# First mixer of a two-block network on Trainium2: token products moved between the steps of the triangular inverse

## The chip, the cores and the metric

The kernel is one program on one core of a Trainium2 chip. The metric is the device time of one execution in microseconds (us), given as a median of several runs. The core's engines run side by side, each through its own queue in order: PE (TensorE, matrix products and transposes into PSUM banks of 512 floats in each of 128 partitions), DVE (VectorE), ACT (ScalarE), POOL (GpSimd) and SP (which only issues transfers here). They wait for each other through semaphores. PE's clock stands at one of two levels, 1.2 and 2.4 GHz; a profile calls the share granted 0.50 and 1.00.

## What is computed

Two networks run one after the other on 256 tokens of width 1024. In the first, each of two layers has a feed-forward block, a mixer, and a second feed-forward block; the second network has two layers of another mixer and a retrieval block. The change is in the mixer of the first network, which runs twice in an execution. Cut to what matters here:

```
proj = u @ w_in        # 3.5 k columns: m (4 heads of 64), r (4 of 64), g (4 of 128), gates
h_m = mlstm(mq, mk, mv, i, f);  y_m = head_rmsnorm(h_m) * sigmoid(mo)
h_r = retention(rope(rq), rope(rk), rv);  y_r = head_rmsnorm(h_r) * silu(rg)
qkv = silu(causal_dwconv(concat(gq, gk, gv), g_conv))          # four taps
q, k = l2norm(q), l2norm(k)
# gated delta rule, in chunks, for every head:
a_mat = eye + where(strict, (kb @ k.T) * decay, 0)             # unit lower triangular
sol = triangular_solve(a_mat, [v * beta, kb * exp(g)])
u = sol_v - sol_k @ S
o = (q * exp(g)) @ S + ((q @ k.T) * decay) @ u
S = exp(g_last) * S + (k * exp(g_last - g)).T @ u
y_g = head_rmsnorm(o) * silu(gz)
out = concat(y_m, y_r, y_g) @ w_out
```

## The kernel before

The kernel works in chunks of 128 tokens (two, index `b`), so the inverse has 4 heads x 2 chunks = 8 matrices of 128 x 128, kept side by side and handled in two halves of four.

**Weights** come as units of 128 x 1024 floats. SP loads unit n into one of three `ring` slots once DVE is done with unit n-3. ACT copies it to a high part (L405) as soon as PE is done with unit n-3, and DVE subtracts to get the low part (L408). PE multiplies high x high, high x low and low x high in a fast format. The `Splitter` calls `split.upto(n)` in the code of ACT and DVE say where in each queue a unit is split; a job that stands behind such a call waits until the unit's turn comes.

**PSUM**: four banks `W` are shared in strict rotation by all numbered jobs (`Group`, `claim`, `freed`): job k may start only when the reader of job k-4 has freed the bank. Four more banks, `ACC`, hold the sums of the down and output projections and lie idle in the rest of the mixer. The list `MIX1_STAGES` gives the names of the stages in order with how many jobs and units each has.

**Order of the mixer**: transposed input (`xT`), small gate columns (`small`), 16 units of channel-major products (`tt0` to `tt3`: m queries and keys, g queries, keys, values, PE L668), with the four-tap convolution of the 12 g tiles on DVE (L1584, L1586, L1588) behind them; 16 units of token-major products (`tok0` to `tok3`, PE L743) in the `W` banks; between them the sums of squares of the g queries and keys (`gss`, L803), roots on ACT (L1203), reciprocals and scaling on DVE (L1597, L1599). Then come the m scores and output (`bM`, `msc`, `mout`), the r scores and output (`rtr`, `rsc`, `rout`), transposes of g keys and values (`gtr`), rows spread over partitions (`bg`, `bb`, L815), key and query products (`gkk`), the inverse, its uses (`gout`, L921), and the output projection of 8 units (`wout`, L690).

**The inverse** (`inv`) works in LEVELS = 7 levels on `TI` and its transpose `WI`. At level n POOL multiplies all 8 matrices with a mask (`EL`, L558); PE forms EL x TI, ACT copies it to `XI` (L1268), PE forms both WI x XI and XI x WI (L910), and DVE subtracts the one from `TI` and the other from `WI` (L1696). `TI` and `WI` are both kept up to date by products.

## Time and profile before

| What | us |
|---|---|
| median of 3 runs (lowest to highest) | 3322.17 (3319.99 to 3328.34) |
| time of the profiled execution | 3336.64 |
| its span, first to last instruction | 3334.9 |
| layer 0 mixer, first `xT` transpose to the end of `wout` | 218.62 to 464.22 |
| layer 1 mixer, same | 871.08 to 1119.67 |
| token units of layer 0 | 282.6 to 341.2 |
| from the token units to the `yT` transposes, layer 0 | 343.2 to 435.2 |

A row of a timeline has a start, a duration, the engine, the line, the operation, and in brackets the idle time before it and what ended it. `x48` counts records; an f32 product that is not of the fast format leaves two records.

### The profile page before, as it was taken

What the parts mean: (1) busy time and instruction counts of PE and PEld (TensorE: products, weight loads), DVE (VectorE), ACT (ScalarE), POOL (GpSimd) and SP (SyncE); (2) the same over time, 40 slices, a digit from 0 to 9 for tenths busy, and PEclk for the clock granted to TensorE, in tenths of its full rate; (3) what the DMA queues carried; (4) which work ended last, traced back from release to release, by engine and by line L of the source; (5) the groups of instructions that cost most, each with busy time, mean ns of one, the idle gap of its engine ahead of it and who ended that gap; (6) DMA issues with size and microseconds to landing.
All of it is one profiled execution on the core that took longest, in us unless ns stands there. A gap on an engine that the chain in (4) does not pass through costs nothing.

```text
span 3334.9 us, 58740 instructions
## 1 busy us (share of the span) xinstructions
PE 3099.9 (93%) x20832; PEld 2830.3 (85%) x20832; DVE 2179.9 (65%) x3744; ACT 1533.2 (46%) x2314; POOL 449.3 (13%) x255
## 2 busy tenths in 40 slices
PE   7988889999888898879999999998879999999997
PEld 7987879989878797769999988887769999988886
DVE  4547545555574555566978867777566978867776
ACT  4445244444452444434555545454435555545543
POOL 0001300000013000113850000000103850000000
PEclk9989789999897899889999999999889999999999
DMA  5535025545340355336876567776335876677775
GB/s 198 188 127 164 20 95 183 188 153 187 127 151 1 121 188 164 124 108 180 224 218 182 182 211 241 242 239 214 115 120 178 226 215 182 182 222 240 241 242 167
DMA packets 213006, 579.56 MB, mean 174 GB/s; under 512 B 23728, under 2 KB 88528, under 8 KB 212352
## 3 DMA queue, kind: packets, MB, share of 16 engines
q1 hardware_dynamic: 209216, 562.62, 54.0%
q0 software_dynamic: 3648, 14.99, 1.3%
q8 instruction: 96, 1.57, 0.2%
q14 instruction: 46, 0.38, 0.0%
HBM read 541.34 MB, written 36.18 MB: 173 GB/s over the span
## 4 chain that ended last, share of the span: by engine, by line
PE 76%; POOL 7%; DVE 7%; issue 6%; ACT 3%; DMA 1%; POOLq 0%; SPq 0%; DVEq 0%; ACTq 0%
PE work L668 33%; PE acc L690 31%; POOL wsp L648 6%; PE work L743 5%; PE acc L1064 3%; PE work L910 2%; DVE xsp L1425 1%; DVE wsp L408 1%; ACT wsp L405 1%; PE work L766 1%; DMA ring<-in_stream 0%; PE work L921 0%; DVE h L1456 0%; PE work L842 0%; DVE h L1730 0%
## 5 line engine op out<-in xcount | busy, mean ns | idle before, releaser
L668 PE MATMUL work<-xsp,wsp 128*128 128x256 f32 x12096 | 1510.6, 285 | 13.9 <-DVE xsp L1425 6.8
L668 PEld LDWEIGHTS work<-xsp,wsp 128*128 128x128 f32 x12096 | 1481.2, 193 | 24.4 <-issue 15.9
L408 DVE TENSOR_TENSOR wsp<-ring,wsp 128x1024 fp32r<-128x1024 f32 x824 | 1010.9, 1227 | 645.7 <-ACT wsp L405 645.2
L405 ACT ACTIVATE wsp<-ring 128x1024 fp32r<-128x1024 f32 x944 | 993.6, 1053 | 601.1 <-PE work L668 275.7
L690 PE MATMUL acc<-wsp,hsp 128*128 128x512 f32 x4128 | 957.8, 391 | 11.2 <-issue 10.9
L690 PEld LDWEIGHTS acc<-wsp,hsp 128*128 128x128 f32 x4128 | 773.4, 189 | 169.4 <-issue 12.0
L648 POOL TENSOR_TENSOR wsp<-ring,wsp 128x1024 fp32r<-128x1024 f32 x120 | 304.4, 2549 | 168.7 <-ACT wsp L405 168.3
L1367 ACT ACTIVATE hsp<-arena 128x256 fp32r (+1 forms) x256 | 107.0, 418 | 360.2 <-PE acc L690 340.3
L529 POOL TENSOR_TENSOR st<-st,mhalf 128x2 f32<-128x2 f32 x12 | 13.3, 1105 | 1689.7 <-DVE st L1440 879.0
L743 PE MATMUL work<-wsp,xsp 128*128 128x512 f32 x768 | 196.0, 417 | 35.5 <-DVE wsp L408 10.7
L743 PEld LDWEIGHTS work<-wsp,xsp 128*128 128x128 f32 x768 | 154.3, 204 | 75.7 <-DVE wsp L408 13.7
L1935 DVE TENSOR_TENSOR one_hots<-iota,selT 128x512 bf16<-128x512 bf16 x256 | 97.2, 422 | 81.7 <-PE acc L1064 81.7
L1973 DVE TENSOR_TENSOR hsp<-arena,hsp 128x256 fp32r<-128x256 f32 x256 | 109.0, 426 | 57.4 <-ACT hsp L1367 57.4
L1944 DVE TENSOR_TENSOR one_hots<-one_hots,selT 128x512 bf16<-128x512 bf16 x384 | 139.6, 420 | 0.0
L1146 ACT ACTIVATE hsp<-scratch 128x256 fp32r<-128x256 f32 x88 | 36.7, 418 | 184.7 <-DVE scratch L1473 184.7
L1962 DVE TENSOR_TENSOR arena<-arena,back 128x256 f32 (+1 forms) x252 | 105.7, 419 | 22.1 <-DMA back<-acts_dram 22.0
L1138 ACT ACTIVATE scratch<-work 128x256 f32<-128x256 f32 x88 | 33.7, 383 | 167.4 <-PE work L668 167.4
L1064 PE MATMUL acc<-one_hots 128*128 128x128 bf16 x1536 | 110.2, 219 | 0.2 <-DVE one_hots L1944 0.2
L690 PE MATMUL acc<-wsp,xsp 128*128 128x512 f32 x384 | 95.5, 413 | 5.6 <-DVE xsp L1425 5.6
L679 PE MATMUL work<-cst,scratch 128*128 128x128 f32 x160 | 37.0, 425 | 67.0 <-DVE scratch L1445 47.9
L690 PEld LDWEIGHTS acc<-wsp,xsp 128*128 128x128 f32 x384 | 77.2, 202 | 23.7 <-issue 7.1
L1064 PEld LDWEIGHTS acc<-one_hots 128*128 128x128 bf16 x1536 | 88.0, 97 | 5.9 <-DVE one_hots L1944 0.4
(301 smaller groups left out, 1950.5 us busy)
## 6 DMA issues: line engine op xcount, KB each, us to landing
ring<-in_stream SPq DMA_DIRECT2D x944, 512.0 KB, 3.5
back<-acts_dram SPq DMA_DIRECT2D x252, 128.0 KB, 3.2
acts_dram<-acts SPq DMA_DIRECT2D x128, 128.0 KB, 3.6
acts_dram<-arena SPq DMA_DIRECT2D x124, 128.0 KB, 4.3
rows_sb<-in_rows POOLq DMA_DIRECT2D x10, 512.0 KB, 5.0
h_saved_dram<-h POOLq DMA_DIRECT2D x2, 1024.0 KB, 4.2
h<-h_saved_dram POOLq DMA_DIRECT2D x2, 1024.0 KB, 7.4
scratch<-in_levels POOLq DMA_DIRECT2D x3, 448.0 KB, 4.8
```

The source lines that it names most:

```text
L405: self.eng.activation(dst[:, 0, :], src, ACT.Copy).then_inc(high_done, 1)
L408: self.eng.tensor_tensor(dst[:, 1, :], src, dst[:, 0, :].bitcast(F32), ALU.subtract)\
L648: pool.tensor_tensor(dst[:, 1, :], ring[:, n % RING, :], dst[:, 0, :].bitcast(F32), ALU.subtract) .then_inc(low_done, 1)
L668: mm = pe.matmul(out_, lhsT=w[:, a, 128 * c:128 * c + 128], rhs=xsp[:, b, c, :], start=(c == 0 and n == 0), stop=(c == DC - 1 and n == 2))
L690: mm = pe.matmul(ACC[2 * b + n][:, :], lhsT=act[:, pa, 128 * b:128 * b + 128], rhs=w[:, pw, 512 * n:512 * n + 512], start=(first and m == ...
L743: mm = pe.matmul(G.bank(b)[:, :], lhsT=xsp[:, px, c, 128 * b:128 * b + 128], rhs=w[:, pw, 512 * cc:512 * cc + 512], start=(c == 0 and n == ...
L1064: mm = pe.matmul(ACC[g % 4][:, 128 * t:128 * t + 128], lhsT=slot[:, 0, t // 2, :, t % 2], rhs=slot[:, m, t // 2, :, t % 2], start=(m == 1) ...
L1367: act.activation(hsp[:, j % 2, 0, :], arena[:, bass.ds(it * (6 * T) + j * T, T)], ACT.Copy)\
L1935: ins = tt(slot[:, m], iota2.unsqueeze(1).broadcast_to([P, 2, NKEYS, 2]), spread(g, m), ALU.is_equal)
L1944: ins = tt(slot[:, m], slot[:, 1], spread(g, {1: 2, 2: 3, 3: 4}[m]), ALU.mult)
L1962: tt(a, a, back[j % 4], ALU.mult).then_inc(gated, 1)
L1973: tt(hsp[:, j % 2, 1, :], arena[:, bass.ds(it * (12 * T) + j * T, T)], hsp[:, j % 2, 0, :].bitcast(F32), ALU.subtract).then_inc(act_low, 1)
```

## The change

In words, for each of the two mixers:

- The channel units come in the order keys, values, queries, then m (`ttk`, `ttv`, `ttq`, `ttm`). ACT writes a tile twice: plain, and scaled with the last tap; DVE adds the other three taps.
- The norms of g keys and queries are no longer multiplied into the tiles. Sums of squares are products with one column of ones (`ksum`, `qsum`), POOL takes the power -1/2 of 8 numbers a partition, and the results are factors: in the decay matrix, in `beta`, in the scales with which ACT evicts the transposed keys and values (`kbe`, `vb`, `kd`), and in the last norm of the output. `gss`, the roots and the reciprocals are gone.
- `NT` is formed ahead of the token units, between the channel units.
- A level of the inverse is `mul` (NT x TI, unmasked), a masking on DVE straight from PSUM into `XI`, `add` (WI x XI), and a subtraction from `TI`. `WI` comes from `turn`, 8 transposes of `TI`, copied by ACT. POOL has no part in it. The masks are loaded transposed.
- The 16 token units accumulate in the `ACC` banks, one between two steps of the inverse or the other jobs; ACT takes a finished group of four (`taken`).
- m, r and g work is dealt out between the levels; the transposed output comes in two halves (`yT0`, `yT1`) with four units of the output projection between.

```diff
-MIX1_STAGES = [("xT", 8, 0), ("small", 1, 0), ("tt0", 4, 4), ("cums", 1, 0), ("tt1", 4, 4), ("rows", 1, 0),
-               ("tt2", 4, 4), ("mcols", 1, 0), ("tt3", 4, 4), ("tok0", 2, 4), ("tok1", 2, 4), ("gss", 4, 0),
-               ("tok2", 2, 4), ("tok3", 2, 4), ("bM", 2, 0), ("msc", 4, 0), ("mout", 2, 0), ("rtr", 4, 0), ("rsc", 4, 0),
-               ("rout", 2, 0), ("gtr", 4, 0), ("bg", 2, 0), ("bb", 2, 0), ("gkk", 4, 0),
-               ("inv", 6 * LEVELS - 6, 0), ("gout", 7, 0), ("yT", 8, 0), ("wout", 0, 8)]
+MIX1_STAGES = [("xT", 8, 0), ("small", 1, 0), ("ttk", 4, 4), ("cums", 1, 0), ("ttv", 4, 4), ("rows", 1, 0), ("ksum", 1, 0),
+               ("ttq0", 2, 2), ("bg", 2, 0), ("ttq1", 2, 2), ("mcols", 1, 0), ("brow", 1, 0), ("gkk", 2, 0),
+               ("ttm0", 2, 2), ("bb", 2, 0), ("ttm1", 2, 2), ("tok", 0, 16), ("inv0", 2, 0), ("qsum", 1, 0), ("turn0", 2, 0),
+               ("mul1", 2, 0), ("add1", 2, 0), ("bM", 2, 0), ("turn1", 2, 0),
+               ("mul2", 2, 0), ("add2", 2, 0), ("gtr0", 2, 0), ("turn2", 2, 0),
+               ("mul3", 2, 0), ("add3", 2, 0), ("msc", 4, 0), ("turn3", 2, 0),
+               ("mul4", 2, 0), ("add4", 2, 0), ("gtr1", 2, 0), ("turn4", 2, 0),
+               ("mul5", 2, 0), ("add5", 2, 0), ("rtr", 4, 0), ("mout", 2, 0), ("turn5", 2, 0),
+               ("mul6", 2, 0), ("add6", 2, 0), ("rsc", 4, 0), ("gqk", 2, 0), ("u0", 1, 0), ("uv1", 1, 0), ("wT", 1, 0),
+               ("rout", 2, 0), ("S1", 1, 0), ("u1", 1, 0), ("yT0", 4, 0), ("out0", 1, 0), ("out1", 1, 0), ("wout0", 0, 4),
+               ("yT1", 4, 0), ("wout1", 0, 4)]
...
-            n8 = NT.rearrange("p h b t -> p (h b) t")
-            G = Group(part, "inv")
-            for n in range(LEVELS):
-                if n:
-                    G.ready(pool, inverse_job(n - 1, 0, 1))
-                pool.tensor_tensor(EL, n8, lvl(n).unsqueeze(1).broadcast_to([P, 8, P]), ALU.mult)\
-                    .then_inc(ev("EL_ready"), 1)
-                if n == 0:
-
-                    pool.wait_ge(ev("W_ready"), l + 1)
...
+                def tokens(t):
+
+                    g, i = t // 4, t % 4
+                    if t == 0:
+                        acc_claim(pe, part)
+                    elif i == 0 and g >= 2:
+                        pe.wait_ge(tok_taken, 8 * l + 2 * (g - 1))
+                    w = K.unit(pe, t)
+                    for cc in range(2):
+                        c = 2 * i + cc
+                        for b in range(NB):
+                            for n, (px, pw) in enumerate(PARTS):
+                                mm = pe.matmul(ACC[2 * (g % 2) + b][:, :], lhsT=xsp[:, px, c, 128 * b:128 * b + 128],
+                                               rhs=w[:, pw, 512 * cc:512 * cc + 512],
+                                               start=(c == 0 and n == 0), stop=(c == DC - 1 and n == 2))
+                    mm.then_inc(unit_done, 1)
...
+                def head_sums(name, sq_):
+
+                    G = Group(part, name)
+                    G.claim(pe, 0)
+                    for b in range(NB):
+                        for i in range(4):
+                            mm = pe.matmul(G.bank(0)[:, 4 * b + i:4 * b + i + 1], lhsT=sq_[:, i, 128 * b:128 * b + 128],
+                                           rhs=ones[:, 0:1], start=True, stop=True)
+                    mm.then_inc(job_done, 1)
+
...
+                Group(part, "rows").freed(pe, 0)
+                spread("bg", rows8, 4, 8)
+                channels("ttq1", 2)
+
...
+                G = Group(part, "brow")
+                G.claim(pe, 0)
+                pe.wait_ge(ev("brk_ready"), l + 1)
+                for b in range(NB):
...
+                channels("ttm0", 2)
+                Group(part, "brow").freed(pe, 0)
+                spread("bb", brow, 0, 4)
+                channels("ttm1", 2)
...
+                def turn(n):
+
+                    made = inv0 if n == 0 else Group(part, f"add{n}")
+                    G = Group(part, f"turn{n}")
+                    for half in range(2):
+                        made.freed(pe, half)
+                        G.claim(pe, half)
+                        for m in range(4):
+                            mm = pe.transpose(G.bank(half)[:, 128 * m:128 * m + 128], TI[:, 4 * half + m, :], ident)
+                        mm.then_inc(job_done, 1)
...
+                def mul(n):
+
+                    made = inv0 if n == 1 else Group(part, f"add{n - 1}")
+                    G = Group(part, f"mul{n}")
+                    for half in range(2):
+                        made.freed(pe, half)
+                        G.claim(pe, half)
+                        for m in range(4):
+                            a = 4 * half + m
+                            mm = pe.matmul(G.bank(half)[:, 128 * m:128 * m + 128], lhsT=n8[:, a, :], rhs=TI[:, a, :],
+                                           start=True, stop=True)
+                        mm.then_inc(job_done, 1)
...
+                def add(n):
+
+                    masked, turned, G = Group(part, f"mul{n}"), Group(part, f"turn{n - 1}"), Group(part, f"add{n}")
+                    lhs, rhs = (WI, XI) if n < LEVELS - 1 else (XI, WI)
+                    for half in range(2):
+                        masked.freed(pe, half)
+                        turned.freed(pe, half)
+                        G.claim(pe, half)
+                        for m in range(4):
+                            a = 4 * half + m
+                            mm = pe.matmul(G.bank(half)[:, 128 * m:128 * m + 128], lhsT=lhs[:, a, :], rhs=rhs[:, a, :],
+                                           start=True, stop=True)
+                        mm.then_inc(job_done, 1)
+
...
+                turn(0)
+                mul(1)
+                tokens(1)
+                add(1)
+                spread("bM", mrow, 0, 4)
+                tokens(2)
+                turn(1)
+
+                mul(2)
+                tokens(3)
+                add(2)
+                pe.wait_ge(ev("conv_silu"), 3 * l + 2)
+                keys_values(0)
+                tokens(4)
...
+                    Group(part, "add6").freed(pe, half)
+                    Group(part, "gtr1").freed(pe, half)
+                heads("u0", lambda i: [(WI[:, 2 * i, :], vb[:, i, 0, :])])
...
+                pe.wait_ge(tok_taken, 8 * l + 6)
+                head_out("rout", rp, lambda b, i: tok[:, b, 768 + 64 * i:832 + 64 * i], 64, "rsc")
+                tokens(13)
+                Group(part, "u0").freed(pe, 0)
+                heads("S1", lambda i: [(kd[:, i, :], u0[:, i, :])])
+                tokens(14)
+                Group(part, "wT").freed(pe, 0)
+                Group(part, "S1").freed(pe, 0)
+                heads("u1", lambda i: [(wT[:, i, :], S1[:, i, :])])
+                tokens(15)
+                make_xT(part, y, "yT0", ("half_y", l + 1), 0, 4)
+                for half in range(2):
+                    Group(part, "gqk").freed(pe, half)
+                heads("out0", lambda i: [(QK[:, i, 0, :], u0[:, i, :])])
+                pe.wait_ge(ev("qe_ready"), l + 1)
+                Group(part, "u1").freed(pe, 0)
+                heads("out1", lambda i: [(qe[:, i, :], S1[:, i, :]), (QK[:, i, 1, :], u1[:, i, :])])
+                pe.wait_ge(tok_taken, 8 * (l + 1))
+                G = Group(part, "wout0")
+                for c in range(4):
+                    down_unit(G, c, xsp[:, :, c, :], c == 0, False)
+                make_xT(part, y, "yT1", ("y_ready", l + 1), 4, 4)
+                G = Group(part, "wout1")
...
+                def channel(name, q, tile):
+
+                    G = Group(part, name)
+                    split.upto(G.u + q + 2)
+                    G.ready_unit(act, q)
+                    src = G.bank(q)[:, 0:T]
+                    act.activation(cin[:, tile, 3:3 + T], src, ACT.Copy)
+                    G.free(act.activation(cT[:, tile, :], src, ACT.Copy,
+                                          scale=pr1[:, l, P_CONV + 4 * tile + 3:P_CONV + 4 * tile + 4]), q)
...
+                def turned(n):
+
+                    G = Group(part, f"turn{n}")
                     for half in range(2):
-                        job = inverse_job(n, 0, half)
-                        G.ready(act, job)
-                        G.free(act.activation(XI[:, 4 * half:4 * half + 4, :].rearrange("p a t -> p (a t)"),
-                                              G.bank(job)[:, :], ACT.Copy), job)
...
+                def conv(name, q, tile):
+
+                    G = Group(part, name)
+                    split.upto(G.u + q + 2)
+                    G.freed(dve, q)
+                    for tap in range(3):
+                        w = pr1[:, l, P_CONV + 4 * tile + tap:P_CONV + 4 * tile + tap + 1]
+                        ins = stt(cT[:, tile, :], cin[:, tile, tap:tap + T], w, cT[:, tile, :], ALU.mult, ALU.add)
+                        if tap < 2:
+                            step(ins)
+                    ins.then_inc(ev("conv_done"), 1)
...
+                conv("ttq1", 0, 2)
+                dve.wait_ge(ev("dec_exp"), 2 * l + 2)
+                for a in range(4):
+                    for b in range(NB):
+                        ins = stt(dec[:, a, b, :], dec[:, a, b, :], kn[:, b, a:a + 1], tri, ALU.mult, ALU.mult)
+                step(ins)
+                conv("ttq1", 1, 3)
...
+                G.ready(dve, 0)
+                G.free(tt(guard, cs[:, :, 0:4], G.bank(0)[:, 0:8].rearrange("p (b n) -> p b n", b=NB), ALU.add), 0)
+                G.freed(dve, 0)
+                dve.tensor_copy(guard, guard).then_inc(ev("mm_ready"), 1)
+                G = Group(part, "brow")
+                G.ready(dve, 0)
+                G.free(dve.tensor_copy(brow[0:4, :], G.bank(0)[0:4, 0:T]), 0)
...
+                def masked(n):
+
+                    for G, half, o, a in halves(f"mul{n}"):
+                        G.free(tt(XI[:, a, :], o, lvl(n).unsqueeze(1).broadcast_to([P, 4, P]), ALU.mult), half)
+
+                def subtract(n):
+
+                    buf = TI if n < LEVELS - 1 else WI
+                    for G, half, o, a in halves(f"add{n}"):
+                        if n == LEVELS - 1:
+                            Group(part, "turn5").freed(dve, half)
+                        G.free(tt(buf[:, a, :], buf[:, a, :], o, ALU.subtract), half)
```

How the instructions stand, first on PE at the token units. Before, L743 is a token unit's product (12 to a unit, so 8 units in a row of 96), L803 the sums of squares, L815 a spread, L829 and L830 the m scores:

```order
L668 MATMUL work<-xsp,wsp 128x256 x96
L743 MATMUL work<-wsp,xsp 128x512 x96
L803 MATMUL work<-scratch,cst 128x512 x4
L743 MATMUL work<-wsp,xsp 128x512 x96
L815 MATMUL work<-scratch,cst 128x256 x4
L829 MATMUL work<-scratch 128x256
```

In the changed kernel L859 makes the transposes of `inv0`, L755 is a token unit's product, L796 `qsum`, L873 a `turn`, L885 a `mul`, L899 an `add`, L811 a spread:

```order
L859 MATMUL work<-cst,scratch 128x128 x8
L755 MATMUL acc<-wsp,xsp 128x512 x12
L796 MATMUL work<-cst,scratch 128x1 x8
L873 MATMUL work<-cst,scratch 128x128 x8
L885 MATMUL work<-scratch 128x128 x8
L755 MATMUL acc<-wsp,xsp 128x512 x12
L899 MATMUL work<-scratch 128x128 x8
L811 MATMUL work<-scratch,cst 128x256 x4
L755 MATMUL acc<-wsp,xsp 128x512 x12
L873 MATMUL work<-cst,scratch 128x128 x8
L885 MATMUL work<-scratch 128x128 x8
```

The token units have moved from two blocks of eight ahead of everything to single ones between the jobs of the inverse. Next, DVE behind the last channel units. Before, L408 is a unit's low part, L1575 the reader of `mcols`, and the others the four taps:

```order
L1586 SCALAR_TENSOR_TENSOR scratch<-scratch 128x256 x2
L1588 SCALAR_TENSOR_TENSOR scratch<-scratch 128x256
L408 TENSOR_TENSOR wsp<-ring,wsp 128x1024
L1575 TENSOR_TENSOR scratch<-scratch,work 128x8
L1577 COPY scratch<-scratch 128x8
L1584 TENSOR_SCALAR scratch<-scratch 128x256
L1586 SCALAR_TENSOR_TENSOR scratch<-scratch 128x256 x2
L1588 SCALAR_TENSOR_TENSOR scratch<-scratch 128x256
```

In the changed kernel L416 is the low part, L1723 the three taps, L1774 the eight differences of the decay, L1781 its eight maskings, L1787 the reader of `mcols` and L1792 that of `brow`, whose banks the first unit behind them (`ttm0`) uses:

```order
L416 TENSOR_TENSOR wsp<-ring,wsp 128x1024
L1723 SCALAR_TENSOR_TENSOR scratch<-scratch 128x256 x3
L1774 TENSOR_SCALAR scratch<-work,scratch 128x128 x8
L416 TENSOR_TENSOR wsp<-ring,wsp 128x1024
L1723 SCALAR_TENSOR_TENSOR scratch<-scratch 128x256 x3
L1781 SCALAR_TENSOR_TENSOR scratch<-scratch,cst 128x128 x8
L416 TENSOR_TENSOR wsp<-ring,wsp 128x1024
L1723 SCALAR_TENSOR_TENSOR scratch<-scratch 128x256 x3
L416 TENSOR_TENSOR wsp<-ring,wsp 128x1024
L1787 TENSOR_TENSOR scratch<-scratch,work 128x8
L1789 COPY scratch<-scratch 128x8
L1792 COPY scratch<-work 4x256
```

The reader of `mcols` now stands behind the decay work. Last, PE from the first g results to the output projection. Before, L910 is the inverse, L921 its uses, L679 the eight transposed tiles, L690 the output projection:

```order
L890 MATMUL work<-cst,scratch 128x128 x8
L910 MATMUL work<-scratch 128x128 x136
L921 MATMUL work<-scratch 128x128 x32
L679 MATMUL work<-cst,scratch 128x128 x16
L690 MATMUL acc<-wsp,xsp 128x512 x96
```

In the changed kernel L1002 makes the uses of the inverse, L755 token units, L661 transposes, L672 the output projection:

```order
L755 MATMUL acc<-wsp,xsp 128x512 x12
L1002 MATMUL work<-scratch 128x128 x4
L755 MATMUL acc<-wsp,xsp 128x512 x12
L1002 MATMUL work<-scratch 128x128 x4
L755 MATMUL acc<-wsp,xsp 128x512 x12
L661 MATMUL work<-cst,scratch 128x128 x8
L1002 MATMUL work<-scratch 128x128 x12
L672 MATMUL acc<-wsp,xsp 128x512 x48
L661 MATMUL work<-cst,scratch 128x128 x8
L672 MATMUL acc<-wsp,xsp 128x512 x48
```

The transposes and the output projection are in two halves now, the first ahead of the last two g products.

## Rows read from the trace of the kernel before

**Rows 1.** The page: shares by engine, then the splitting of weights on DVE and ACT.
```profile
PE 3099.9 (93%) x20832; PEld 2830.3 (85%) x20832; DVE 2179.9 (65%) x3744; ACT 1533.2 (46%) x2314; POOL 449.3 (13%) x255
...
L408 DVE TENSOR_TENSOR wsp<-ring,wsp 128x1024 fp32r<-128x1024 f32 x824 | 1010.9, 1227 | 645.7 <-ACT wsp L405 645.2
L405 ACT ACTIVATE wsp<-ring 128x1024 fp32r<-128x1024 f32 x944 | 993.6, 1053 | 601.1 <-PE work L668 275.7
```
**Rows 2.** Stretches of layer 0: length, busy PE, PEld, DVE, ACT, POOL, granted clock, DMA, GB/s.
```profile
282.60:341.20 58.60, 49.74 (x202) 38.10 (x200) 39.69 (x31) 35.62 (x41) 8.99 (x6) 0.97 0.48 152
343.20:435.20 92.00, 76.95 (x497) 71.55 (x497) 45.75 (x99) 21.53 (x68) 30.37 (x18) 0.77 0.02 7
354.00:366.00 12.00, 10.48 (x51) 9.39 (x51) 6.11 (x20) 2.46 (x12) 2.42 (x3) 0.50 0.01 1
405.00:422.00 17.00, 16.63 (x147) 16.44 (x146) 8.75 (x14) 3.58 (x6) 5.64 (x3) 1.00 0.01 2
```
**Rows 3.** Timeline of PE, layer 0: transposes and weight units.
```profile
218.62 3.71 PE L679 MATMUL work<-cst,scratch 128*128 128x128 f32 x16 [6.37 <-DVE scratch L1445]
...
231.91 13.64 PE L668 MATMUL work<-xsp,wsp 128*128 128x256 f32 x96
...
247.36 11.75 PE L668 MATMUL work<-xsp,wsp 128*128 128x256 f32 x96 [0.80 <-DVE wsp L408]
...
312.86 11.13 PE L743 MATMUL work<-wsp,xsp 128*128 128x512 f32 x48 [1.31 <-ACT scratch L1203]
328.74 12.55 PE L743 MATMUL work<-wsp,xsp 128*128 128x512 f32 x48 [4.75 <-issue]
...
435.20 3.71 PE L679 MATMUL work<-cst,scratch 128*128 128x128 f32 x16 [4.17 <-DVE scratch L1524]
440.31 23.91 PE L690 MATMUL acc<-wsp,xsp 128*128 128x512 f32 x96 [1.39 <-DVE xsp L1425]
```
**Rows 4.** Timeline of PE, layer 0: small jobs of the mixer.
```profile
341.22 1.99 PE L815 MATMUL work<-scratch,cst 4*128 4x256 f32 x8
...
349.06 2.42 PE L842 MATMUL work<-scratch 128*128 128x65 f32 x10 [1.24 <-DVE scratch L1622]
...
357.96 1.23 PE L829 MATMUL work<-scratch 64*128 64x256 f32 x4 [0.83 <-ACT scratch L1246]
...
366.12 0.42 PE L866 MATMUL work<-cst,scratch 128*128 128x128 f32 x1
...
369.32 0.27 PE L867 MATMUL work<-cst,scratch 128*128 128x128 f32 x1
```
**Rows 5.** Timeline of PE, layer 1.
```profile
871.08 3.61 PE L679 MATMUL work<-cst,scratch 128*128 128x128 f32 x16 [6.35 <-DVE scratch L1445]
...
1039.68 1.10 PE L890 MATMUL work<-cst,scratch 128*128 128x128 f32 x8 [2.93 <-POOL scratch L558]
...
1095.75 23.92 PE L690 MATMUL acc<-wsp,xsp 128*128 128x512 f32 x96 [1.39 <-DVE xsp L1425]
```
**Rows 6.** Timeline of DVE, layer 0.
```profile
251.32 1.01 DVE L1586 SCALAR_TENSOR_TENSOR scratch<-scratch 128x256 f32<-128x256 f32 x2
...
371.49 2.16 DVE L1654 TENSOR_SCALAR scratch<-work,scratch 128x128 f32<-128x128 f32 x8 [1.99 <-ACT scratch L1257]
...
393.41 0.69 DVE L1696 TENSOR_TENSOR scratch<-scratch,work 128x512 f32<-128x512 f32 x1 [7.30 <-PE work L910]
394.30 0.69 DVE L1696 TENSOR_TENSOR scratch<-scratch,work 128x512 f32<-128x512 f32 x1 [0.20 <-PE work L910]
```
**Rows 7.** Timeline of POOL, layer 0: one masking of a level.
```profile
403.55 2.36 POOL L558 TENSOR_TENSOR scratch<-scratch 128x1024 f32<-128x1024 f32 x1 [3.07 <-PE work L910]
```
**Rows 8.** Timeline of ACT, layer 0: a table load, two activations of 128x1024.
```profile
240.23 1.28 ACT L1185 ACT_TABLE_LOAD   x1
...
298.11 2.01 ACT L1225 ACTIVATE scratch<-scratch 128x1024 f32<-128x1024 f32 x2
```

785 lines of the change are left out of this document (422 added, 363 removed).

## Prediction

> **What bounds the kernel now.** I read the page's shares first: PE is busy 93% of the span, so whatever shortens the time must take work or waiting from PE or raise its clock [rows 1]. The change touches only the first mixer, run twice, so the next view is the table of stretches of one mixer, and there the page's average misleads. In the token units (58.6 us) PE is at clock 0.97 and loaded with weights. In the 92.0 us behind them no weight arrives (DMA share 0.02), the clock is 0.77, and POOL is busy for 30 us. PE counts as busy for 77 us there, but part of that is at half clock: in 354 to 366 PE is busy 10.5 of 12 us at 0.50, with small products only; in 405 to 422, the products of the inverse, it is at 1.00 [rows 2]. The timeline of PE then gives the ends of a mixer: 218.62 to 440.31 + 23.91 = 464.22, so 245.6 us in layer 0, and 871.08 to 1095.75 + 23.92 = 1119.67, so 248.6 us in layer 1 [rows 3, 5]. The timelines of DVE and POOL show the loop of a level: a POOL masking of 2.36 us with 3.07 us of waiting before it, that is one level in 5.4 us [rows 7]. Of these 5.4 us PE's 24 products fill nearly all at full clock: the DVE subtractions of 0.69 us start 0.89 us apart, one job of four products each, so a product costs 0.22 us [rows 6]. The inverse is bound by PE already; what is wasted is clock and gaps around it, and the 8 products a level that only keep the transpose of `TI`.
>
> **The change: PE's work at full clock.** I rebuild a mixer as what PE must do one after the other, and add the waits afterwards.
>
> - `xT` and `small`, unchanged: 218.62 to 231.91 = 13.3 us [rows 3].
> - 16 channel units: 13.5 us for the first four, which start at low clock, then 11.75 / 4 = 2.94 each for 12 = 35.2; sum 48.7 [rows 3].
> - Between them: `cums` with its wait to the next unit as now (up to 247.36) 2.0; `rows`, `mcols`, `brow` 0.3 each = 0.9, an estimate from two transposes; `bg` and `bb` 1.99 each like `bM`, 4.0 [rows 4]; `gkk` 8 products of 0.22 = 1.8 [rows 6]. `ksum` is 8 products of one column. Nothing in the rows has that shape; it can hardly be dearer than 8 spread products of 256 columns (4.0) nor cheaper than the 1.1 of 8 transposes [rows 4, 5]; I take 2.0, near the 128-column product, as loading the weights is the same. Sum 10.7.
> - `inv0`: 8 transposes in 1.10 [rows 5]; `qsum` 2.0 as above. Sum 3.1.
> - 16 token units: 11.13 / 4 = 2.78 each at full clock, 44.5 [rows 3]. That they go to other banks changes nothing in their length.
> - The inverse: 6 `turn` of 1.1 = 6.6; 12 `mul` and `add` of 2 x 0.89 = 21.4 [rows 5, 6]. Sum 28.0, where 34 jobs of 0.89 = 30.3 stood and POOL in the loop.
> - The jobs dealt out between: `bM` 2.0, `gtr` 16 transposes 2.2, `rtr` 1.1, `gqk` 1.8, five of the g uses at 0.9 = 4.5; `mout` and `rout` have 24 records each, 2.42 / 10 = 0.24 a record at half clock, so 2.7 each at full; `msc` and `rsc`: 1.23 for two heads' wide products at half clock and the narrow ones to it, about 2.0 each at full, an estimate [rows 4]. Sum 20.9.
> - `yT0`, `yT1` 2.2, `out0` 0.9, `out1` 1.8. Sum 4.9.
> - 8 output units of the same 12 products of 512 columns as a token unit, 2.78 each = 22.2 (23.91 now, with a start at low clock [rows 3]).
>
> Sum: 13.3 + 48.7 + 10.7 + 3.1 + 44.5 + 28.0 + 20.9 + 4.9 + 22.2 = 196.3 us.
>
> **What PE waits for.** The cover of the inverse's handovers is one token unit of 2.78 us. DVE's masking is 2 x 0.69 [rows 6] behind one low part of 1.23, which itself waits for ACT's 1.05 [rows 1], released by the token unit before: 1.05 + 1.23 + 1.4 = 3.7 us, against the `turn`, `mul` and token unit in between (5.7 us): covered, as is the subtraction behind `add`, which has a small job and a token unit. Uncovered are six places:
>
> - `ksum` waits for the squares of the keys. ACT needs a table load of 1.28, `silu` and square of 1.0 each, and two evictions [rows 8], some 4.5 us against one channel unit of 2.9: 1.5 us.
> - The first `ttm0` unit claims the bank of `mcols`. DVE reads it only after 6 low parts (7.4), 5 convolutions of three taps at 0.5 (7.5) [rows 6], the row copy and scan 1.1, eight differences 2.2 [rows 6], eight maskings of the same size (2.4, an estimate from the differences), a dozen small ones 1.6, and 1.9 of waiting for POOL and ACT: 24.1 us. PE has four units (11.7), `bg`, `mcols`, `brow`, `gkk` (4.4) and about 1.0 of waiting for ACT in the same time and starts 0.8 later: 24.1 - 0.8 - 17.1 = 6.2 us of idle PE. This is the largest single wait, and nothing covers it.
> - `turn0` waits for DVE's four steps at `inv0`: 1.0 us.
> - The rotation of banks. `msc`, `rtr` and `rsc` have four jobs, so their third and fourth need the banks of the `add` just before, freed only by the subtraction, which stands behind a low part: 1.1 + 1.0 + 1.0, and `gqk` behind `rsc` 1.2. Sum 4.3.
> - `yT0` ends with a wait for its four tiles. ACT must first split a unit (1.05) and take the last token group (2 x 0.55), then 4 tiles at about 0.44: 3.6 us beyond the transposes. Now eight tiles at half clock take 435.20 to 440.31, 5.1 us [rows 3].
> - `yT1`: half of these 5.1 us, less its transposes: 1.5 us. The g norm before it (about 6 us on ACT, POOL and DVE) lies beside four output units of 11 us.
>
> Sum 18.1 us. Then the clock. Behind the idle 4.75 us four token units took 12.55 instead of 11.13, and the first channel units 13.64 instead of 11.75 [rows 3]: a fall costs 1.4 to 1.9. I count three falls (`ttm0`, the small jobs around `inv0` and `qsum`, `yT0`) at 2.0 = 6.0. Bounds: none, 0, and one for each of the 12 slots, 24.
>
> A mixer is then 196.3 + 18.1 + 6.0 = 220.4 us. Gain: 245.6 - 220.4 = 25.2 in layer 0 and 248.6 - 220.4 = 28.2 in layer 1, 53.4 us together. The profiled span of 3334.9 goes to 3281.5; against the median of 3322.2, 14 us below the profiled execution, that is **3269 us**.
>
> One rule speaks against this change. In the trace the clock rises in the midst of the 16 transposes of `gtr`: the first takes 0.42 us, the last 0.27 [rows 4]. The Trainium skill (TensorE: Matmul & The Clock Gate, Part 4: PE-mode transpose) says that the clock gate does not take transposes for activity of PE. By that rule the six `turn` would count as pauses. These rows do not bear it out plainly, since work from before may have raised the clock; the time that it would give is the second rival.
>
> **The rivals.**
>
> *Better cover.* The 6.2 us at `ttm0`, the rotation waits and the clock falls are worked out from queues. If they vanish, 5 to 6 us of waiting stay: 196.3 + 5.5 = 201.8 a mixer, gain 43.8 + 46.8 = 91 us, 3232 us. For it: PE's own products set the level period already [rows 6]. Against: DVE is in order, and its work behind the last channel units is plain to count.
>
> *Thin cover.* Each of six levels has a small fall of the clock in or after its `turn`, or a handover that is late by as much: 6 x 2.0 = 12 us a mixer more. Gain 13.2 + 16.2 = 29 us, 3293 us. For it: small products kept the clock at 0.50 for 12 us with PE nearly always busy [rows 2]. Against: in each level there are 5.6 us of token units and 3.6 of products that held 1.00. (By the rule on transposes just named, the trace would look like this.)
>
> *Slower.* The clock stays low in the interleaved stretch. Its work at full clock is 3.1 + 44.5 + 28.0 + 20.9 + 4.9 = 101.4 us, and every share of it at half clock is added once more. From 25% on the gain of 25.2 us is gone; at 40% a mixer is 40.6 - 25.2 = 15 us slower, two of them 28, 3350 us. The place is the stretch from `inv0` to `out1`. For it: 0.50 in [rows 2]. Against: the token units at 0.97 and the inverse at 1.00 [rows 2].
>
> *It does not do what it says:* the token units could turn out to wait in their place, one each, for a low part. DVE has 2 low parts, masking and subtraction, 5.2 us, in a slot of about 11 us, so I see no room for that, and count it under thin cover.
>
> **How the numbers follow.** Forecast (3252 to 3284) 0.53; better cover 0.17; thin cover 0.22; slower 0.05; between these, no change 0.03. The range 3235 to 3303 holds the forecast, all of thin cover but its end, and the nearer half of better cover. A difference of 0.3%, 10 us, is about what a measurement of this kernel can tell from none: faster 0.92, the same 0.03, slower 0.05.
>
> **What would show it.** In the profile of the changed kernel: the mixer from the first transpose to the end of the output projection at about 220 us; POOL without the maskings of 1024 columns; a token unit at 2.8 us between the jobs; levels 11 to 13 us apart, with PE idle under 1 us in each; an idle 6 us ahead of the `ttm0` units, released by DVE's reader of `mcols`; 3 to 4 us of idle PE behind `yT0`; the granted clock above 0.9 from `inv0` to `out1`. The prediction is wrong if levels take 14 us and more, if the clock there is under 0.85, or if the `ttm0` wait is not there or twice as long.

## The result: 3267.7 us, 1.7% faster, and the profile after

The changed kernel takes 3267.69 us (median of 4 runs, 3262.54 to 3270.03), the kernel before, measured with it, 3324.48 us (4 runs, 3319.99 to 3328.34). The ratio is 0.9828 with a 95% interval of 0.9808 to 0.9847. The prediction said 3269.

First the page of the changed kernel, its line of engines (to be held against [rows 1]): POOL has lost 40 us and DVE 45, and PE, which bounds the kernel, 45.

```profile
PE 3055.3 (93%) x20820; PEld 2800.7 (86%) x20820; DVE 2134.5 (65%) x3718; ACT 1535.3 (47%) x2356; POOL 409.5 (13%) x235
```

Both mixers from the first transpose to the end of the output projection, in the table of stretches (length, then busy PE, PEld, DVE, ACT, POOL, granted clock, DMA share, GB/s). Of the kernel before:

```profile
218.62:464.22 245.60, 218.12 (x1278) 193.71 (x1278) 142.05 (x228) 101.59 (x177) 39.36 (x24) 0.86 0.26 84
871.08:1119.67 248.59, 221.49 (x1278) 195.91 (x1278) 141.99 (x228) 101.40 (x177) 39.31 (x24) 0.85 0.26 83
```

Of the changed kernel:

```profile
219.27:439.29 220.02, 203.07 (x1272) 183.99 (x1272) 120.55 (x215) 103.64 (x199) 19.77 (x14) 0.91 0.29 94
844.85:1067.27 222.42, 203.91 (x1272) 184.94 (x1272) 120.73 (x215) 103.47 (x199) 19.79 (x14) 0.91 0.28 93
```

The gain is 25.6 us in layer 0 and 26.2 in layer 1, 51.8 together, in one trace each. The medians differ by 56.8 us and the two traces by 67.0 (3334.9 and 3267.9). What is over 51.8 lies in code that did not change, whose length moves from trace to trace: 2840.7 us in that of the kernel before, 2825.5 in that of the changed kernel, 2821 to 2834 in those of the experiments. So single runs below are read by their mixers, not by their whole time. In layer 0, PE's idle time went from 27.5 us (245.60 - 218.12) to 17.0. Its busy time fell by 15.0, and that is mostly the clock, by an estimate from the table: at 0.86 of full clock 14% of 245.6 us is lost, 34 us, and at 0.91 9% of 220, 20 us, so 14 less. The number of PE's records hardly moved (1278 and 1272).

Where much of it came from is seen in the stretches of the kernel before behind its token units: the small jobs, then the inverse (the columns are those of the table above).

```profile
341.20:383.40 42.20, 35.48 (x161) 30.67 (x160) 25.70 (x69) 12.15 (x39) 6.39 (x5) 0.63 0.04 14
383.40:421.70 38.30, 35.63 (x280) 34.95 (x280) 17.03 (x25) 7.16 (x12) 21.97 (x11) 0.87 0.01 1
```

80 us at 0.63 and 0.87, the inverse with two waits for POOL at its start, in PE's timeline of before:

```profile
383.41 1.97 PE L890 MATMUL work<-cst,scratch 128*128 128x128 f32 x8 [2.94 <-POOL scratch L558]
387.97 33.66 PE L910 MATMUL work<-scratch 128*128 128x128 f32 x272 [2.59 <-POOL scratch L558]
```

In the changed kernel the same kinds of jobs stand between token units, and 54 us on end run at 1.00, with 1.4 us of idle PE (first row). What is left of low clock are islands, two of them in the other rows:

```profile
307.00:361.00 54.00, 52.58 (x343) 46.80 (x344) 31.16 (x45) 25.72 (x49) 12.49 (x8) 1.00 0.29 93
363.00:376.50 13.50, 12.50 (x69) 10.87 (x69) 3.20 (x5) 4.12 (x9) 0.00 (x0) 0.75 0.13 40
...
408.70:413.90 5.20, 5.14 (x25) 5.17 (x25) 0.17 (x1) 1.51 (x8) 1.01 (x1) 0.50 0.17 65
```

PE's timeline of the changed kernel, layer 0 (start, length, engine, line, operation, then the idle time before it and its releaser), is to be held against [rows 3, 4]:

```profile
262.58 1.95 PE L796 MATMUL work<-cst,scratch 128*128 128x1 f32 x16 [1.52 <-ACT scratch L1306]
264.39 7.48 PE L649 MATMUL work<-xsp,wsp 128*128 128x256 f32 x48
...
287.38 7.49 PE L649 MATMUL work<-xsp,wsp 128*128 128x256 f32 x48 [3.85 <-DVE scratch L1787]
...
296.72 6.02 PE L649 MATMUL work<-xsp,wsp 128*128 128x256 f32 x48
...
322.86 2.97 PE L755 MATMUL acc<-wsp,xsp 128*128 128x512 f32 x12
...
340.70 0.70 PE L921 MATMUL work<-scratch 64*128 64x256 f32 x2 [1.42 <-DVE scratch L1831]
...
364.48 0.44 PE L980 MATMUL work<-cst,scratch 128*128 128x128 f32 x2 [0.84 <-DVE scratch L1831]
...
368.86 5.27 PE L755 MATMUL acc<-wsp,xsp 128*128 128x512 f32 x12
...
408.76 5.46 PE L1002 MATMUL work<-scratch 128*128 128x128 f32 x24 [3.63 <-DVE xsp L1598]
```

`ksum` waits 1.52 us. The first `ttm0` unit waits 3.85 for the reader of `mcols` (5.32 in layer 1). The pairs of channel units at 264.39 and 287.38 take 7.5 us where the pair at 296.72 takes 6.02. A token unit takes 2.97, but the one behind `mout` 5.27. The products behind `yT0` wait 3.63 and then run at half clock.

### The profile page after: what moved, and what is told of

Read it like the earlier page. It is cut to its first block, busy times and chain, and to the rows that moved or that the text cites. A ratio compares the mean times of both kernels' runs of the same rounds, so it can differ in the third digit from the quotient of the medians.

```text
span 3267.9 us, 58680 instructions
## 1 busy us (share of the span) xinstructions
PE 3055.3 (93%) x20820; PEld 2800.7 (86%) x20820; DVE 2134.5 (65%) x3718; ACT 1535.3 (47%) x2356; POOL 409.5 (13%) x235
## 4 chain that ended last, share of the span: by engine, by line
PE 78%; DVE 7%; POOL 6%; issue 6%; ACT 3%; DMA 0%; POOLq 0%; SPq 0%; DVEq 0%; ACTq 0%
PE work L649 34%; PE acc L672 32%; POOL wsp L629 6%; PE acc L755 3%; PE acc L1162 3%; PE work L725 2%; DVE xsp L1598 1%; DVE wsp L416 1%; PE work L885 1%; ACT wsp L413 1%; PE work L1002 1%; PE work L766 1%; DVE h L1629 0%; DVE h L1960 0%; DVE h L1954 0%
## 5 line engine op out<-in xcount | busy, mean ns | idle before, releaser
L416 DVE TENSOR_TENSOR wsp<-ring,wsp 128x1024 fp32r<-128x1024 f32 x824 | 1010.9, 1228 | 691.0 <-ACT wsp L413 690.8
L672 PE MATMUL acc<-wsp,hsp 128*128 128x512 f32 x4128 | 955.5, 391 | 9.2 <-issue 9.2
L672 PEld LDWEIGHTS acc<-wsp,hsp 128*128 128x128 f32 x4128 | 771.8, 188 | 166.7 <-issue 9.5
L725 PE MATMUL work<-wsp,xsp 128*128 128x512 f32 x384 | 97.5, 416 | 17.4 <-DVE scratch L2008 8.3
L725 PEld LDWEIGHTS work<-wsp,xsp 128*128 128x128 f32 x384 | 76.9, 202 | 36.5 <-DVE scratch L2008 9.0
L755 PE MATMUL acc<-wsp,xsp 128*128 128x512 f32 x384 | 100.5, 413 | 0.0
L672 PE MATMUL acc<-wsp,xsp 128*128 128x512 f32 x384 | 93.4, 405 | 6.4 <-DVE xsp L1598 6.4
L672 PEld LDWEIGHTS acc<-wsp,xsp 128*128 128x128 f32 x384 | 75.2, 197 | 23.5 <-issue 7.6
```

The lines of the kernel that those rows point to most:

```text
L416: self.eng.tensor_tensor(dst[:, 1, :], src, dst[:, 0, :].bitcast(F32), ALU.subtract)\
L672: mm = pe.matmul(ACC[2 * b + n][:, :], lhsT=act[:, pa, 128 * b:128 * b + 128], rhs=w[:, pw, 512 * n:512 * n + 512], start=(first and m == ...
L725: mm = pe.matmul(G.bank(b)[:, :], lhsT=xsp[:, px, c, 128 * b:128 * b + 128], rhs=w[:, pw, 512 * cc:512 * cc + 512], start=(c == 0 and n == ...
L755: mm = pe.matmul(ACC[2 * (g % 2) + b][:, :], lhsT=xsp[:, px, c, 128 * b:128 * b + 128], rhs=w[:, pw, 512 * cc:512 * cc + 512], start=(c == ...
```

## The experiments

The theory at the outset was the prediction's: token units are the cover that the inverse's handovers need. Its rival: there is less to do and wait for (POOL's maskings, the bigger products, the waits between the old token blocks), and where the token units stand is indifferent. The first four kernels are the changed kernel with one edit each.

One thing has to be known before mixers are compared. Ahead of `inv0`, where e1, e2 and e4 change nothing, layer 0 of the changed kernel took 83.4 us (302.65 - 219.27), but its layer 1 and both layers of e1, e2 and e4 took 85.7 to 86.0: the units of `ttv` ran slower there (13.2 us, not 11.74), and `ttm0` waited longer. Likewise the fall of the clock at `mout` (3.2 us, of which 2.3 in the token unit behind it) is in both layers of the changed kernel, but not in e2 and e3, which have no edit near it. A difference of 2 to 3 us between two mixers is therefore not the edit's until it is found at the edit's place.

**e1: all sixteen token units ahead of `turn0`, fifteen of them in one row.** The other jobs stay between the levels of the inverse.

```diff
                 head_sums("qsum", gsqq)
+                for t in range(1, 16):
+                    tokens(t)
...
                 mul(1)
-                tokens(1)
                 add(1)
```

> All 16 token units stand ahead of the first turn and run one behind the other, as in the kernel before; every other job keeps its place. The changed kernel's mixers take 220.0 and 222.4 us. Theory (the token units cover the handovers of the inverse): with nothing to do between mul and add, PE waits about 0.9 us for the second half of the masking and 0.9 us for the subtraction in each of six levels, more where a small job's reader stands in DVE's queue, and small jobs alone let the clock fall: 12 to 20 us a mixer more, 232 to 240 us, and 24 to 40 us in the whole time, 3292 to 3308. Rival (the gain is less work: no root, no reciprocals, transposes for products; the place of the token units is indifferent): mixers 220 to 224 us, time within 5 us of 3268.

Measured: 3264.13 us (3261.6 to 3269.5), ratio to before 0.9822 (0.9791 to 0.9853); mixers of 219.4 and 219.3 us against 220.0 and 222.4. The theory falls in this form. The table of stretches of e1, from behind the row of token units to the end of the mixer:

```profile
350.48:437.56 87.08, 78.90 (x544) 70.91 (x542) 48.99 (x89) 35.34 (x94) 5.65 (x5) 0.96 0.15 49
```

The levels have waits of 0.16 to 0.41 us only, and there is no fall of the clock at `mout`. A second reading of this comes with e10.

**e2: the products of before in place of five transposes.** `WI` is kept by a product and a subtraction.

```diff
-                turn(1)
+                wadd(1)
...
-                turned(1)
+                subtract_w(1)
```

> In levels 1 to 5 the transposed inverse WI is kept up to date by a product and a subtraction on DVE, as in the kernel before, in place of 8 transposes and a copy by ACT. Theory: 8 products take 1.78 us where 8 transposes take 0.9 to 1.0, five times: 4 us a mixer more, 224 and 226 us; DVE's 1.4 us more in each level are hidden by the token units. Rival (transposes count as a pause for PE's clock): without them the clock does not fall behind mout (the token unit there takes 5.27 us in place of 2.83), and the mixers take 221 us or less. Second rival: DVE is the tighter queue and its 1.4 us are not hidden: 228 us and more.

Measured: 3269.49 us (one run); mixers of 222.9 and 222.7 us, 2.9 and 0.2 more. Eight products take 1.78 us where eight transposes take 0.87, so five should cost 4.6 more. From `inv0` on, and without the 3.2 us at `mout`, both layers are 3.5 us longer: the wait at `msc` was 0.50 us instead of 1.42, which gives back 0.9. The other 2.5 us of layer 0 lie ahead of `inv0`. At `mout` there was no fall (the token unit behind it took 3.02 us, not 5.27). If that has nothing to do with the edit (e3, which keeps the transposes, has no fall there either), the transposes are worth 3.5 us a mixer; if it has, 0.3. One run can't tell, and either is a small part of the gain.

**e3: the readers of `mcols` and `brow` ahead of DVE's last convolution.**

```diff
-                conv("ttq1", 1, 3)
-                split.upto(Group(part, "ttm0").u + 2)
                 G = Group(part, "mcols")
...
+                conv("ttq1", 1, 3)
+                split.upto(Group(part, "ttm0").u + 2)
```

> DVE reads mcols and brow right behind the eight maskings of the decay, ahead of the low part and the convolution that it now does first. Theory (the idle time ahead of the ttm0 units is DVE's queue in front of the reader of mcols, and the two units behind it are slow because the clock fell in it): the idle 3.85 and 5.32 us fall under 0.8, the pair of units takes 5.9 in place of 7.5 and 8.4, mixers of about 215.5 us both, time 12 us shorter. Rival (the queue as a whole is too full; the wait comes back at bb or inv0): mixers 218 to 222 us, idle time at the spread bb or at inv0.

Measured: 3256.26 us (one run); mixers of 210.5 and 212.5 us, 9.5 and 9.9 less, where I expected 4.5 and 7. (The whole time fell by 11.4 us, as expected: the unchanged rest of this trace was 6 us longer.) PE's timeline of e3 at `ttm0`:

```profile
284.02 6.01 PE L649 MATMUL work<-xsp,wsp 128*128 128x256 f32 x48 [0.24 <-DVE scratch L1785]
...
291.89 6.02 PE L649 MATMUL work<-xsp,wsp 128*128 128x256 f32 x48
...
363.11 3.01 PE L755 MATMUL acc<-wsp,xsp 128*128 128x512 f32 x12
```

The wait is 0.24 us instead of 3.85, and the pair behind it runs at full clock (6.01 instead of 7.49). That is 5.1 us in layer 0. The other 4.4 lie far behind: 3.2 at `mout`, whose token unit took 3.01 us (last row), and 1.2 at the products behind `yT0` and the output units behind them; layer 1 has the same two. They are low clock that is gone, but that the edit took it away is not shown, since in e2 there was no fall at `mout` either. (The first q units took 5.99 us, not 7.48, but the `ttv` units ahead of them were slower by as much.) In the whole mixer PE was idle for 3.6 us less and busy for 6.0 less. So the removed wait was worth itself and 1.5 us of low clock right behind it; the rest came with it in this trace.

**e4: `mout` behind the token unit.**

```diff
+                tokens(10)
                 pe.wait_ge(tok_taken, 8 * l + 4)
                 head_out("mout", pm, lambda b, i: vaug[:, b, i, :], 65, "msc")
-                tokens(10)
```

> Token unit 10 is moved ahead of mout, so it stands between the rtr transposes (with two waits of together 1.0 us) and the 24 narrow records of mout. In the changed kernel the clock falls in mout, token unit 10 takes 5.27 us in place of 2.83, and mout itself is slower by about 1 us. Theory (the fall comes from waits, transposes and narrow products in a row, 5.8 us without wide products): split by a token unit the clock stays high, mixers 3 to 3.5 us shorter, 216.6 and 219. Rival (mout lets it fall by itself): the fall moves on to turn 5 and mul 6, which together take 5 us and more in place of 2.8, and the mixers stay within 1 us.

Measured: 3262.02 us (one run); mixers of 219.4 and 219.2 us, 0.6 and 3.2 less. There is no fall at `mout` (token unit 3.02 instead of 5.27), and from `inv0` on both layers are 3.2 us shorter, as expected. That the edit did it is likely, not shown, since e2 and e3 had no fall there without it. In layer 0 the second token unit starts 94.1 us into the mixer instead of 91.5: 1.5 of these 2.6 us were lost in the `ttv` units (13.24 us, not 11.74), the rest at `ttm0`, all ahead of the edit. PE's timeline of e4 has this at `ttm0`:

```profile
274.62 6.02 PE L649 MATMUL work<-xsp,wsp 128*128 128x256 f32 x48
288.28 8.55 PE L649 MATMUL work<-xsp,wsp 128*128 128x256 f32 x48 [5.32 <-DVE scratch L1787]
```

The pair ahead was at full clock here (6.02, not 7.50), and the wait is longer by the 1.5 us that it gained (5.32, not 3.85), as in layer 1 of the changed kernel. From the first q unit to `ttm0` it is 23.0 us in all three: DVE sets when `mcols` is read, and PE, being faster, only waits longer, with lower clock behind (8.55, not 7.49).

After e1 the gain needed another reason. The new theory: small jobs are cheap where they stand between products that need nothing of them, and costly when they stand together, since there each waits for the reader of the last and the clock falls over them. The rival stayed POOL.

**e7: all small jobs gathered ahead of `turn0`, the inverse bare.** Otherwise e1.

```diff
+                spread("bM", mrow, 0, 4)
...
+                head_scores("msc", mqk, 0, 2)
...
+                head_scores("rsc", rT, 0, 2)
...
+                keys_values(1)
                 turn(0)
                 mul(1)
                 add(1)
-                spread("bM", mrow, 0, 4)
                 turn(1)
```

> The sixteen token units stand ahead of the inverse, as in e1 (mixers 219.4 and 219.3 us), and now the dense small jobs (bM, msc, mout, rtr, rsc and both transposes of g) stand gathered ahead of turn0 too, so the twelve products and five of the six turns of the inverse follow each other bare, as in the kernel before. Nothing is left out and nothing added. Theory (what makes the mixer shorter is that other products of PE stand between a product of the inverse and the one that needs it, whatever they are): each level then waits for DVE's and ACT's steps, about 1 to 1.5 us a level or 5 to 8 us in all, and the gathered narrow jobs and the waits take the clock down for some 15 to 25 us, 8 to 12 us more; a mixer of 232 to 240 us, the clock below 0.9 in the stretch behind the token units. Rival (the gain is that POOL's maskings of 2.36 us are off the path and that there is less to do; the place of the jobs is indifferent): within 3 us of e1, 217 to 222 us a mixer.

Measured: 3287.04 us (one run); mixers of 232.4 and 230.7 us, 13.0 and 11.4 over e1, with no work added (11.7 in layer 0 without what lies ahead of `inv0`): about half of the change's gain. The stretches of e7, the gathered jobs and then the bare inverse:

```profile
350.42:371.40 20.98, 17.08 (x89) 14.84 (x88) 9.38 (x23) 8.18 (x17) 0.00 (x0) 0.67 0.15 51
371.77:404.39 32.62, 29.82 (x240) 27.27 (x241) 15.88 (x23) 10.69 (x27) 0.00 (x0) 1.00 0.00 1
```

The number is at the theory's lower end, but not for all of its reasons: I had laid 5 to 8 us of waiting on the bare levels, and PE is idle for 2.8 us in them. One level, from turn to turn (two halves of a turn, `mul`, `add`):

```profile
378.56 0.60 PE L876 MATMUL work<-cst,scratch 128*128 128x128 f32 x4
379.50 0.66 PE L876 MATMUL work<-cst,scratch 128*128 128x128 f32 x4 [0.34 <-DVE scratch L1801]
380.00 1.95 PE L888 MATMUL work<-scratch 128*128 128x128 f32 x16
381.84 2.05 PE L902 MATMUL work<-scratch 128*128 128x128 f32 x16
383.78 0.66 PE L876 MATMUL work<-cst,scratch 128*128 128x128 f32 x4
```

A bare level takes 5.2 us at clock 1.00. Most of the cost seems to be in the 21 us ahead of it, at 0.67; e12 looks at that.

**e8: POOL masks again.** The order is the changed kernel's, but for the first token unit, which stands ahead of `inv0` here; POOL masks the transpose for each level, and ACT takes the product away.

```diff
-                            mm = pe.matmul(G.bank(half)[:, 128 * m:128 * m + 128], lhsT=n8[:, a, :], rhs=TI[:, a, :],
+                            mm = pe.matmul(G.bank(half)[:, 128 * m:128 * m + 128], lhsT=EL[:, a, :], rhs=TI[:, a, :],
...
-                masked(1)
```

> The order of PE's work is that of the changed kernel (mixers 220.0 and 222.4 us), but POOL masks the transpose for each level again, as in the kernel before (seven maskings of 1024 columns a mixer, 2.36 us each in its trace), PE multiplies with the masked copy, and ACT, not DVE, takes the products away unmasked. Nothing of the computation is left out. Theory (with other products between the steps of the inverse a masking on POOL is hidden, since a slot is about 11 us long): mixers within 3 us of the changed kernel, 219 to 225 us, POOL busy for some 35 us a mixer instead of 20. Rival (POOL's maskings were what lengthened the levels before, so that taking them away is the gain): 2.36 us a level come back in part or whole, six levels, 14 us: 232 us and more.

Measured: 3280.27 us (one run); mixers of 226.3 and 223.3 us, 6.3 and 0.9 more; POOL busy for 37.5 us. Layer 0 is above the theory's end and below the rival's 232. PE's timeline of e8 names the places:

```profile
288.20 8.56 PE L664 MATMUL work<-xsp,wsp 128*128 128x256 f32 x48 [5.32 <-DVE scratch L1818]
...
308.42 1.09 PE L876 MATMUL work<-cst,scratch 128*128 128x128 f32 x8 [1.03 <-POOL scratch L545]
...
346.31 0.70 PE L938 MATMUL work<-scratch 64*128 64x256 f32 x2 [2.47 <-DVE scratch L1862]
```

The first masking delays `inv0` by 1.03 us, with lower clock in `turn0` and `mul1` behind it, 2.7 us together. The wait at `msc` grew by 1.05. That at `ttm0` and the pair behind it grew by 1.5 and 1.1, but so they did in e4, without POOL. No product of the levels 1 to 6 waits for POOL. Layer 1 has the same 2.7 and 1.05; its total is only 0.9 over because it had no fall at `mout` (and 1.6 us of low clock behind `msc` instead). So the maskings are worth some 3.7 us a mixer in this order, not the gain. What they cost in the order of before, where they stood in a bare loop, no run isolates.

**e12: the inverse bare, the small jobs dealt out between token units.** e7 did two things at once; this one keeps the inverse bare and undoes the gathering. It is built on e9 (below).

```diff
                 tokens(4)
...
+                head_scores("msc", mqk, 0, 2, range(2))
                 tokens(5)
+                head_scores("msc", mqk, 0, 2, range(2, 4))
                 tokens(6)
...
+                keys_values(0)
...
                 turn(0)
                 mul(1)
                 add(1)
                 turn(1)
```

> e7 gathered the small jobs and left the inverse bare at once, so it does not say which of the two cost its 12 us. This kernel takes e9 (mixers 205.8 us), leaves the inverse bare (turn, mul, add, turn, ... with nothing between), but deals the small jobs (bM, msc, both gtr, rtr, mout, rsc) out one by one between the token units. Theory now (small jobs cost when they stand together, since they wait for each other's readers and the clock falls over them; the inverse needs nothing between its steps, e7's levels took 5.17 us at clock 1.00 with 0.24 us of waiting each): 204 to 208 us a mixer, the levels 5.2 us apart, the clock 1.00 from the first token unit to the last level. Rival (products between the steps of the inverse are what the gain rests on): 210 us and more, with waits of over 0.5 us in each level.

Measured: 3251.24 us (3250.0 to 3255.9), ratio 0.9790 (0.9763 to 0.9816); mixers of 212.1 and 214.2 us, 6.3 and 8.5 over e9. From `inv0` on it is 6.4 in both layers, all of it ahead of `gqk`; the other 2.1 of layer 1 lie ahead of `inv0`. My numbers are missed, and the rival's are met, though not with its waits. PE's timeline of e12, the start of the bare levels:

```profile
352.36 1.81 PE L874 MATMUL work<-cst,scratch 128*128 128x128 f32 x8 [1.91 <-DVE scratch L1864]
353.96 2.89 PE L886 MATMUL work<-scratch 128*128 128x128 f32 x16
356.69 2.10 PE L900 MATMUL work<-scratch 128*128 128x128 f32 x16
...
363.85 0.66 PE L874 MATMUL work<-cst,scratch 128*128 128x128 f32 x4
364.74 0.66 PE L874 MATMUL work<-cst,scratch 128*128 128x128 f32 x4 [0.24 <-DVE scratch L1830]
365.24 1.95 PE L886 MATMUL work<-scratch 128*128 128x128 f32 x16
```

And the same three jobs in e9, with a token unit between:

```profile
314.38 1.03 PE L873 MATMUL work<-cst,scratch 128*128 128x128 f32 x8
315.25 1.95 PE L885 MATMUL work<-scratch 128*128 128x128 f32 x16
316.96 2.98 PE L755 MATMUL acc<-wsp,xsp 128*128 128x512 f32 x12
319.78 1.95 PE L899 MATMUL work<-scratch 128*128 128x128 f32 x16
```

There turn and `mul` take 316.96 - 314.38 = 2.58 us and `add` 1.8 to 1.9, 4.5 together, against 5.2 for a bare level: 0.7 us a level, 4 us a mixer. PE's column of idle time shows only 0.24 of it; the rest is the end of each half, counted busy. To it come the wait of 1.91 ahead of `turn0`, low clock behind it (1.7) and 0.5 at `rsc`, less the 2.4 of waits at `msc` and `rtr` that this order does not have: 5.7 of the 6.3 us in layer 0. So both halves of e7 cost: the bare levels about 4 us, and, as the rest of its 12, the gathering of the small jobs some 8.

**e9: four edits together.** e3, e4, `ksum` behind the first two q units, and PE's wait for the `yT0` tiles behind `out0` and `out1`.

```diff
-                make_xT(part, y, "yT0", ("half_y", l + 1), 0, 4)
+                make_xT(part, y, "yT0", ("half_y", l + 1), 0, 4, False)
...
+                for q in range(4):
+                    Group(part, "yT0").freed(pe, q)
                 G = Group(part, "wout0")
```

> Four edits to the order of the changed kernel, each aimed at one of its waits: the readers of mcols and brow ahead of the last convolution on DVE (e3: mixers 210.5 and 212.5 us), mout behind the token unit (e4: less than 1 and 3 us), ksum behind the first two q units so that the squares are ready (its wait of 1.52 us and the clock low in it), and PE's wait for the four yT0 tiles put behind out0 and out1, with the last token group taken by ACT ahead of its last split (a wait of 3.63 us and a product stretch at half clock of 2.6). Theory (the waits and the clock falls behind them add up, each at its own place): 211.5 less 1.5 to 3 less 3 to 5: mixers of 203 to 207 us, 3238 to 3248 us in all. Rival (a wait removed lets the clock fall at another place, as e4 did, so that little is left of it): 209 to 213 us, 3252 to 3258 us.

**e10: the same, but the token units in one row.** The lines of e1 on top of e9 (`mout` stands where it did).

```diff
                 head_sums("qsum", gsqq)
+                for t in range(1, 16):
+                    tokens(t)
```

> The same edits as e9 (readers ahead, ksum later, PE's wait for yT0 behind out0 and out1), but all sixteen token units in one row ahead of the inverse, as in e1. If the place of the token units is indifferent, as e1 against the changed kernel says (219.4 against 220.0, 219.3 against 222.4 us), this is within 3 us a mixer of e9. If they cover something once the other waits are gone (the wait for yT0, whose inputs must come from ACT), it is slower than e9 by 3 us a mixer or more.

Measured: e9 3240.20 us (3234.6 to 3247.4), ratio 0.9759 (0.9737 to 0.9781), mixers of 205.8 and 205.8 us; e10 3247.40 us (3243.6 to 3259.3), ratio 0.9781 (0.9752 to 0.9810), mixers of 209.8 and 212.4. The stretch of e9 from `inv0` to the end of the mixer:

```profile
296.75:424.19 127.44, 122.22 (x761) 107.02 (x760) 73.11 (x113) 57.60 (x123) 18.15 (x13) 1.00 0.32 104
```

The waits add up as forecast, and the clock is 1.00 for 127 us. And e10 adds to e1: with the large waits gone, dealing out the token units is worth 4.0 and 6.7 us a mixer in the traces (4.6 in layer 1 from `inv0` on). The times are not cleanly apart (the intervals overlap), so this rests on one trace each, whose two layers agree. The place is not the inverse. From `qsum` to `gqk` e10 takes 84.6 us with fifteen token units, e9 74.3 with eleven; at 2.73 us each in the row the four more are 10.9, so e10 is 0.6 us faster there. From `gqk` to the `yT0` transposes it takes 12.1 us, e9 20.0 with four token units: 3.0 slower. From there to `yT1` it is 1.7 slower (2.2 in layer 1). PE's timeline of e10 behind `gqk`:

```profile
393.46 1.13 PE L992 MATMUL work<-scratch 128*128 128x128 f32 x8 [0.73 <-issue]
396.55 1.06 PE L661 MATMUL work<-cst,scratch 128*128 128x128 f32 x8 [1.96 <-DVE scratch L1669]
398.13 4.54 PE L992 MATMUL work<-scratch 128*128 128x128 f32 x24 [0.52 <-DVE xsp L1579]
```

And the last of them in e9:

```profile
396.51 2.92 PE L1002 MATMUL work<-scratch 128*128 128x128 f32 x24 [0.52 <-DVE xsp L1601]
```

So in these traces the units that cover something are the last four, between the uses of the inverse. Between its steps the small jobs do as well as the token units. In e1 the same 3.0 us were hidden: the changed kernel lost 3.2 at `mout`, and 2.1 more than e1 behind `yT0`, where e1 waited 1.87 us instead of 3.63.

**e11: three more waits behind other work.** On e9: `msc` and `rtr` in halves with a token unit between, `yT1` ahead of the last unit of `wout0`.

```diff
-                for c in range(4):
+                for c in range(3):
                     down_unit(G, c, xsp[:, :, c, :], c == 0, False)
-                make_xT(part, y, "yT1", ("y_ready", l + 1), 4, 4)
+                make_xT(part, y, "yT1", ("y_ready", l + 1), 4, 4, False)
+                down_unit(G, 3, xsp[:, :, 3, :], False, False)
```

> The kernel of e9 (mixers 205.8 and 205.8 us, 3240.2 us) with three waits of PE more put behind work that needs nothing of them: the four msc products in two halves with a token unit between (its wait of 1.44 us), the four rtr transposes likewise (0.84 and 0.16 us), and the second half of the transposed y ahead of the last unit of the first half of the output projection, with PE's wait for the tiles behind that unit (1.84 us). Theory (waits add up, each at its own place, as long as the clock does not fall elsewhere): 205.8 less 4.3 is 201.5 us a mixer, some 3231 us in all. Rival (the clock's falls move, or y's second half is not ready a unit earlier, so that PE waits there instead): 204 to 206 us a mixer, 3236 to 3242 us.

Measured: 3232.19 us (5 runs, 3226.5 to 3238.1), ratio to before 0.9721 (0.9698 to 0.9745); mixers of 200.3 and 201.7 us, where 201.5 was expected. The stretches of e11:

```profile
217.88:418.21 200.33, 194.01 (x1272) 176.59 (x1272) 120.47 (x215) 103.19 (x199) 19.94 (x14) 0.95 0.32 103
827.35:1029.07 201.72, 195.59 (x1272) 178.01 (x1272) 120.74 (x215) 103.32 (x199) 19.93 (x14) 0.94 0.32 102
```

PE is idle for 6.3 us a mixer instead of 17.0, with the changed kernel's own work: 35 us less than it.

## Why the prediction was right, and where it was not

**The mixer.** Forecast: 220.4 us. Measured: 220.0 and 222.4. Work and clock, 196.3 + 6.0 = 202.3, stand against 203.1 and 203.9 of busy PE; waits of 18.1 against 17.0 and 18.5 of idle PE, which holds two waits more than I had listed.

**The work at full clock** is borne out best by e9, where from `inv0` to the end the clock was 1.00: 122.2 us busy, and the terms of the sum for it are 3.1 + 44.5 + 28.0 + 20.9 + 4.9 + 22.2 = 123.6. `ksum` and `qsum`, whose shape no row had, took 1.84 to 1.95 (2.0 forecast). A turn takes 0.87 from start to start, not 1.1. Token units take 2.83 (2.78). One term was worked out wrongly: 24 records at half of 0.24 us are 2.9, not 2.7; `mout` took 2.6 at full clock.

**The waits**, in layer 0, forecast and then measured: `ksum` 1.5, 1.52. `ttm0` 6.2, 3.85 (5.32 in layer 1): the right place and releaser, with the row of DVE's work too long by 0.9 to 2.4 us. `turn0` 1.0, none. `msc`, `rtr`, `rsc`, `gqk` 1.1, 1.0, 1.0, 1.2 against 1.42, 1.00, 0.42, none. `yT0` 3.6, 3.63. `yT1` 1.5, 1.80. Sum 18.1 against 13.6. To it come 1.93 behind `cums` (hidden in my 2.0 for the jobs there, 3.1 in fact) and 1.37 at `small`, which I had in the unchanged part.

**The clock** was the term that was too small. Three falls at 2.0 were forecast. Measured: three pairs of channel units at 7.5 instead of 6.0 (4.4), the end of `mout` (0.9) and the token unit behind it (2.3), `yT0`'s products and the units behind them (3.0): 10.6 us. Two of my places were right, `ttm0` and `yT0`; around `inv0` and `qsum` nothing fell, and at `mout`, which I had at full clock, it did. The 4.6 us too few here and the 4.5 us too many in the waits cancelled, which was luck: without it the forecast would have been 4 to 5 us a mixer off, still inside its range.

**The reason.** I wrote that the inverse was bound by PE and what was wasted was clock and gaps around it. That was borne out: idle PE -10.5 and clock -14. What I called the cover was not. I took the token unit as what hides the handovers of the inverse; e1 and e10 show that without it the stretch with the inverse loses nothing, as long as small jobs stand between the levels. Token units are worth some 5 us a mixer at another place, behind `gqk` (e10). Levels with nothing at all between their steps do cost (e12: 6.4 us a mixer, with the wait ahead of the first). Larger is what standing together costs the small jobs: with that and a bare inverse, e7 gives back 12 us, about half of the gain. The other half I can read but did not isolate, and its cause stays open: the waits of 1.31 and 4.75 us in [rows 3] are gone, as are the 2.94 and 2.59 us of waiting for POOL, and fewer products stand in the inverse.

**The signs that I named.** The clock from `inv0` to `out1` was 0.94, the `ttm0` wait stood in its place, POOL's maskings were gone. But I had called the prediction wrong if levels took 14 us and more. The distances of the turns in both layers were 12.1, 10.8, 14.0, 10.8 and 18.1 us: the third level holds `msc` with its wait of 1.42, the fifth `rtr`, `mout` and the fall. By my own terms the fifth, with `rtr`, `mout` and two token units, comes to 15 us, so the bound was too tight; 3.2 of the 18.1 us are the fall, which I did not have there.

**The rivals.** Thin cover (3293): no level had a fall in or after its turn; the one in the fifth stands ahead of it. Slower (3350): the clock in the interleaved stretch was 0.94. Better cover (3232): not in this kernel, but it is what e11 gave, 3232.2, once DVE's and PE's orders were put right.

**The rule on transposes.** The levels of the changed kernel ran at 1.00 for 54 us with five turns of eight transposes in them, and e7's bare levels for 32.6 us, with 0.9 of each 5.2 us in transposes. The Trainium skill (TensorE: Matmul & The Clock Gate, Part 4: PE-mode transpose) says that they do not count as activity of PE. No run here holds transposes alone for long, so none contradicts it; but turns of 0.9 us between products cost no clock, and the rival that the rule would have fed did not come. In e2, with five of the turns replaced by products, there was no fall at `mout`, but nor was there one in e3, which has them.

## What to carry to other kernels

Do not look for cover only where a chain of products waits for its handovers: deal the small, narrow jobs out one by one between other products that need nothing of them, since together they wait for each other's readers, with the clock at 0.67 (e7). Price a removed wait as itself plus the slower work right behind it (e3: 3.6 us of wait and 1.5 of the pair), and place an engine's wait for a result as late as the first instruction that reads it. When an order is tested by moving one thing, test it again with the largest waits removed, as the first answer can be hidden by them, and compare stretch by stretch: a total that moved by 3 us may have moved where nothing was edited.

## What the runs showed of the hardware

- Behind the four `rtr` transposes with waits of 0.84 and 0.16 us and `mout`'s products of 65 columns, the clock fell in both layers of the changed kernel and in layer 0 of e8: the token unit there took 5.27 to 5.35 us instead of 3.0. With the same instructions between `add5` and it, it did not fall in e2, e3 and layer 1 of e8 (3.00 to 3.02 us). With a token unit directly ahead of `mout`, in e4 and e9, it did not fall either. The first ten records of `mout` took 1.22 to 1.23 us in the changed kernel, e4, e9 and e12, and 2.42 in e7, where they stood among other small jobs.
- So where the clock falls is not set by the jobs at that place alone. Another case: in e4, and in layer 1 of the changed kernel, the pair of units ahead of `ttm0` ran at full clock (6.02 us, not 7.50), with no edit near it, and the `ttv` units ahead at less (13.24, not 11.74).
- A product of one column costs nearly as much as one of 128: 16 records of 128x1 in 1.84 us, 16 of 128x128 in 1.95.
- A bare chain of f32 products and transposes over two halves of 512 columns each, with DVE and ACT in every handover, ran at clock 1.00 with 0.24 to 0.34 us of visible waiting in 5.2 us (e7).
